# A chunked recurrence on five engines: loads moved to SyncE, six places for levels, a root by logarithm, sums in halves

## What is computed

```python
def step(state, xs):
    qt, kt, vt, bt = xs            # bt: cumulated log of the forget gate
    rel = jnp.where(tri, bt[:, :, :, None, :] - bt[:, :, None, :, :], -jnp.inf)
    att = jnp.einsum('bhtd,bhsd,bhtsd->bhts', qt, kt, jnp.exp(rel))
    o = jnp.einsum('bhts,bhsv->bhtv', att, vt) + \
        jnp.einsum('bhtd,bhdv->bhtv', qt * jnp.exp(bt), state)
    b_last = bt[:, :, -1:, :]
    new_state = jnp.exp(b_last[:, :, 0, :])[..., None] * state + \
        jnp.einsum('bhsd,bhsv->bhdv', kt * jnp.exp(b_last - bt), vt)
    return new_state, o
...
o_b = rms_norm(hgrn2(bq, bf, bi, lb_all[j]), b_out_norm_g[j])
o_b = o_b * jax.nn.silu(bg)
mix = jnp.concatenate([o_a, o_b], axis=-1) @ even_w_out[j]
x = x + mix
```

## Time and profile before

| what | us |
|---|---|
| median of 3 runs (2735.41 to 2735.88) | 2735.71 |
| the profiled execution, its own time | 2738.51 |
| its span in the profile | 2736.8 |
| TensorE busy (share of the span) | 2499.5 (91%) |
| VectorE busy | 1589.1 (58%) |
| GpSimd busy | 1353.6 (49%) |
| ScalarE busy | 1051.3 (38%) |
| from ScalarE's last attention copy to its first exponential of the loop (678.82 to 703.81) | 25.0 |
| first level to own projection (703.81 to 896.02) | 192.2 |

### The profile page before, as it was taken

The page is one execution under the profiler, slowest core; times in us unless marked ns, Lnnn a source line. Parts: engine busy times, 40 slices in busy tenths (PEclk is TensorE's granted clock), DMA queues, the critical chain, the costliest instruction groups (busy, mean ns, idle before and its releaser), DMA issues.

```text
span 2736.8 us, 31345 instructions
## 1 busy us (share of the span) xinstructions
PE 2499.5 (91%) x11111; PEld 1985.3 (73%) x11133; DVE 1589.1 (58%) x2354; ACT 1051.3 (38%) x1741; POOL 1353.6 (49%) x770
## 2 busy tenths in 40 slices
PE   6898897788577899999999989988998999999999
PEld 4677676444576678888888877766776888888887
DVE  6478668883677544455544654656534455544472
ACT  4255687555343422232322144525443232322220
POOL 4101234886555065566655913227524566655591
PEclk8999898799789999999999999988989999999999
DMA  4211123000300111122111212112002222111211
GB/s 147 50 28 28 31 66 93 12 10 3 123 9 8 31 55 38 61 62 61 47 38 38 74 73 73 45 33 81 9 16 62 62 61 61 46 39 38 61 54 69
DMA packets 164002, 136.57 MB, mean 50 GB/s; under 512 B 22969, under 2 KB 137730, under 8 KB 163906
## 3 DMA queue, kind: packets, MB, share of 16 engines
q1 hardware_dynamic: 143058, 116.19, 14.1%
q10 hardware_dynamic: 20848, 19.14, 2.4%
HBM read 116.17 MB, written 13.63 MB: 47 GB/s over the span
## 4 chain that ended last, share of the span: by engine, by line
PE 72%; DVE 9%; issue 8%; ACT 4%; POOL 3%; ACTq 1%; DMA 0%; another core or an unknown queue 0%; DVEq 0%; POOLq 0%
PE ps L2130 21%; PE ps L2132 21%; PE ps L2131 21%; ACT signs L1200 1%; POOL diag L824 1%; PE ps L2325 1%; PE ps L2242 1%; DVE ub L2023 1%; PE ps L2485 1%; POOL cl L874 1%; PE ps L2313 1%; PE ps L2333 1%; DVE ps L1709 1%; POOL w_lo L709 1%; DVE shared L2020 1%
## 5 line engine op out<-in xcount | busy, mean ns | idle before, releaser
L2130 PE MATMUL ps<-h_hi,w_hi 128*128 128x512 f32 x1680 | 671.6, 400 | 13.6 <-POOL w_lo L727 9.7
L2131 PE MATMUL ps<-h_lo,w_hi 128*128 128x512 f32 x1680 | 660.0, 393 | 0.0
L2132 PE MATMUL ps<-h_hi,w_lo 128*128 128x512 f32 x1680 | 659.5, 393 | 0.0
L2130 PEld LDWEIGHTS ps<-h_hi,w_hi 128*128 128x128 f32 x1680 | 319.9, 190 | 83.1 <-issue 14.4
L2131 PEld LDWEIGHTS ps<-h_lo,w_hi 128*128 128x128 f32 x1680 | 320.0, 190 | 68.2 <-issue 3.9
L709 POOL TENSOR_TENSOR w_lo<-w_raw,w_hi 128x1024 fp32r<-128x1024 f32 x73 | 182.6, 2501 | 377.3 <-ACT w_hi L1210 374.8
L2132 PEld LDWEIGHTS ps<-h_hi,w_lo 128*128 128x128 f32 x1680 | 319.1, 190 | 67.9
L2020 DVE TENSOR_TENSOR x_res<-ps,x_res 128x1024 f32<-128x1024 f32 x224 | 268.8, 1221 | 115.5 <-PE ps L2132 115.5
L2001 DVE TENSOR_TENSOR u_all<-ps,u_all 128x512 f32<-128x512 f32 x112 | 77.4, 691 | 415.9 <-ACT u_all L1107 415.9
L727 POOL TENSOR_TENSOR w_lo<-w_raw,w_hi 128x1024 fp32r<-128x1024 f32 x112 | 266.8, 2401 | 104.0 <-ACT w_hi L1096 104.0
L2130 PE MATMUL ps<-w_hi,uo_hi 128*128 128x512 f32 x784 | 307.5, 392 | 2.4 <-DVE shared L2020 2.4
(11 more groups left out here) (345 smaller groups left out, 4548.7 us busy)
## 6 DMA issues: line engine op xcount, KB each, us to landing
w_raw<-in_mlp_w_up SPq DMA_DIRECT2D x64, 512.0 KB, 4.0
w_raw<-in_mlp_w_down SPq DMA_DIRECT2D x64, 512.0 KB, 3.8
w_raw<-in_even_w_in SPq DMA_DIRECT2D x23, 512.0 KB, 3.8
w_raw<-in_odd_w_in SPq DMA_DIRECT2D x10, 512.0 KB, 3.7
x_res<-in_x SPq DMA_DIRECT2D x8, 512.0 KB, 8.1
x_res<-in_x ACTq DMA_DIRECT2D x8, 512.0 KB, 8.6
scr_x<-x_res SPq DMA_DIRECT2D x8, 512.0 KB, 2.6
x_res<-scr_x SPq DMA_DIRECT2D x8, 512.0 KB, 4.4
```

Source lines behind the costliest of these rows:

```text
L2130: t_.matmul(out_, ah, bh, start=first, stop=False)
L2131: t_.matmul(out_, ah, bl, start=False, stop=False)
L2132: return t_.matmul(out_, al, bh, start=False, stop=last)
```

## The change

- **Loads.** SyncE issues the value and gate loads and those of `x`, tiles 0 to 6, once the last attention values are multiplied and the sources are saved; tile 7 of `x` follows when all levels are done.
- **The last attention block** is divided in VectorE's slot 6, copied in ScalarE's slot 9, subtracted in GpSimd's slot 11. VectorE starts its loop when the attention's logits are done, TensorE at once.
- **Six places.** `RING` is 6: places 4 and 5 (`cl2`) lie where tile 7 of `x` goes. `READ_LAG` is 5.
- **Distances.** Output and state product at 4, root at 6, turn at 8, state at 9, gate at 12, high at 13, low at 14. `klT` is copied and `qe` made in the next chunk's first slots; the loop has 71 slots.
- **Root.** ScalarE makes four squares with an accumulated sum, Ln, Exp with scale -0.5, and the four scalings from bank 5, in one piece. VectorE's sum, reciprocal and norm are gone.
- **Sums.** The turned keys go to bank 7, so bank 4 holds only sums. Each of the 16 sums is made in two halves (6 matmuls) in adjacent slots; it is added four slots after its first half.

```diff
-        RING = 4
-        cl = at("cl", R_U, [P, RING, 512])
+        RING = 6
+        cl, cl2 = at("cl", R_U, [P, 4, 512]), at("cl2", R_X + 28 * KB, [P, 2, 512])
...
-        L_KL_ARG, L_KL_EXP, L_KL_PROD, L_KL_TURN, L_KL_COPY = 0, 2, 3, 4, 6
-        L_QE_EXP, L_QE_PROD, L_LAST, L_SPLIT = 4, 5, 6, 6
-        R_OUT, R_SQUARE, R_STATE, R_ROOT, R_NORM, R_TURN, R_GATE, R_HIGH, R_LOW = 1, 4, 5, 6, 7, 6, 9, 10, 11
-        READ_LAG = 3
+        L_KL_ARG, L_KL_EXP, L_KL_PROD, L_KL_TURN, L_SPLIT = 2, 3, 4, 5, 6
+        R_KL_COPY, R_QE_EXP, R_QE_PROD, R_LAST = 0, 2, 2, 4
+        R_OUT, R_ROOT, R_STATE, R_TURN, R_GATE, R_HIGH, R_LOW = 4, 6, 9, 8, 12, 13, 14
+        READ_LAG = 5
         HG_SLOTS = 7 * T + R_LOW + 1
+        LAST_NORM, LAST_HIGH, LAST_LOW = 6, 9, 11
...
-        OA_SLOTS = [7 * c + l for c in range(2, T) for l in (0, 2)] + [7 * T + l for l in (0, 2, 4, 5)]
-        OA_LAG = 3
+        OA_FIRST = [7 * c + l for c in range(2, T) for l in (-1, 2)] + [7 * T + l for l in (-1, 2, 5, 8)]
+        OA_PIECES = {n + k // 2: (i, (k, k + 1)) for i, n in enumerate(OA_FIRST) for k in (0, 2)}
+        OA_ADDS = {n + 4: i for i, n in enumerate(OA_FIRST)}
...
+            sp.wait_ge(att["pv_done"], len(TILES[0]))
...
+            for c in range(T):
+                sp.dma_start(chunk_values(o_sum, c), heads(scr_v[:, c, :])).then_inc(chunk_landed(c)[0], 16)
+                sp.dma_start(chunk_values(o_den, c), scr_g[:, :, c * P:(c + 1) * P]).then_inc(chunk_landed(c)[0], 16)
+            for t in range(T - 1):
+                sp.dma_start(x[:, t, :], a["x"][0, t * P:(t + 1) * P, :]).then_inc(x_landed[t], 16)
...
-            act.wait_ge(att["o_lo"], T)
-            act.wait_ge(b_ready, 8)
-            for c in range(T):
-                act.dma_start(chunk_values(o_sum, c), heads(scr_v[:, c, :])).then_inc(chunk_landed(c)[0], 16)
...
                 d = after_chunk(n, R_ROOT)
                 if d is not None:
-                    act.wait_ge(hg["o_ss"], d + 1)
-                    s.activation(sd[:, 0:4], ss[:, 0:4], ACT.Sqrt, scale=1.0 / P, bias=epsc[:]) \
-                        .then_inc(hg["o_sd"], 1)
+                    act.wait_ge(hg["s_done"], d + 1)
+                    for h in range(4):
+                        hs = slice(h * P, (h + 1) * P)
+                        ins = s.activation(kf[:, d, hs], ps[:, 5, hs], ACT.Square, accum_out=ss[:, h:h + 1])
+                    own.link(ins)
+                    own.link(s.activation(sd[:, 0:4], ss[:, 0:4], ACT.Ln, scale=1.0 / P, bias=epsc[:]))
+                    own.link(s.activation(rstd[:, 0:4], sd[:, 0:4], ACT.Exp, scale=-0.5))
+                    for h in range(4):
+                        ins = s.activation(chunk_values(o_sum, d)[:, h, :], ps[:, 5, h * P:(h + 1) * P], ACT.Identity,
+                                           scale=rstd[:, h:h + 1])
+                    ins.then_inc(hg["o_norm"], 1)
...
-            dve.wait_ge(att["o_lo"], T)
+            dve.wait_ge(att["st_done"], len(TILES[0]))
...
-                    v.tensor_reduce(ss[:, 0:4], heads(ps[:, 7, :]), AX_X, ALU.add).then_inc(hg["o_ss"], 1)
-                d = after_chunk(n, R_NORM)
...
-                            ins = t_.transpose(ps[:, 4, hs], ek[:, hs], ident[:])
+                            ins = t_.transpose(ps[:, 7, hs], ek[:, hs], ident[:])
...
-                    for k in range(4):
+                    for k in ks:
                         ins = products(ps[:, 4, :], (h_hi[:, k, ts_], h_lo[:, k, ts_]), (w_hi[:, k, cs], w_lo[:, k, cs]),
                                        k == 0, k == 3)
-                    ins.then_inc(down_done, 1)
+                    if ks[-1] == 3:
+                        ins.then_inc(down_done, 1)
```

More of the change, by code:

```diff
@@ L377, in after_chunk, with level @@
             return c if rem == 0 and 0 <= c < T else None
+        def level(n):
+            return (cl if n % RING < 4 else cl2)[:, n % RING % 4, :]
         def chunk_values(t, c):
@@ L855, in attention @@
                     u = ends_at(layer, n - ROUND[layer])
-                    if u is not None and u % 2:
+                    if u is not None and u % 2 and (layer or u // 2 < T - 1):
                         q = u // 2
@@ L865, in _ @@
             attention(0, PF0, PH0, PL0, diag0)
-            for n in range(7 * T):
+            last_block = block_outputs(0, T - 1)
+            for n in range(7 * T + R_QE_PROD + 1):
                 c, l = divmod(n, 7)
[L868 to L881, removed]
+                if n == LAST_LOW:
+                    pool.wait_ge(att["o_hi"], T)
+                    g.tensor_tensor(h_lo[last_block], o_den[last_block], h_hi[last_block].bitcast(F32), ALU.subtract) \
+                        .then_inc(att["o_lo"], 1)
+                if c < T:
+                    B = 1 << l
+                    e = level(n).rearrange("p (m s j) -> p m s j", s=2, j=B)
+                    pairs = kq[:, 0:2 * (KQ + B)].rearrange("p (s r) -> p s r", s=2)[:, :, c * 512:(c + 1) * 512]
+                    mixed = pairs.rearrange("p s (m j) -> p m s j", j=2 * B)[:, :, :, 0:B]
+                    pool.wait_ge(hg["exp"], 2 * n + 2)
+                    g.tensor_tensor(e, e, mixed, ALU.mult).then_inc(hg["prod"], 1)
+                    if l == L_KL_PROD:
+                        pool.wait_ge(hg["kl_exp"], c + 1)
+                        g.tensor_tensor(ek[:], ek[:], kf[:, c, :], ALU.mult).then_inc(hg["kl"], 1)
+                d = after_chunk(n, R_QE_PROD)
+                if d is not None:
+                    pool.wait_ge(hg["qe_exp"], d + 1)
+                    g.tensor_tensor(qe[:], qe[:], qf[:, d, :], ALU.mult).then_inc(hg["qe"], 1)
+                if l == L_SPLIT and 2 <= c < T and c % 2:
@@ L1324, in round_last @@
                 round_weights(U_OUT0 + 4 + i)
+            last_block = block_outputs(0, T - 1)
             for n in range(HG_SLOTS):
                 c, l = divmod(n, 7)
+                if n == LAST_HIGH:
+                    act.wait_ge(att["o_norm"], T)
+                    s.activation(h_hi[last_block], o_den[last_block], ACT.Copy).then_inc(att["o_hi"], 1)
                 if c < T:
-                    tk, B = slice(c * P, (c + 1) * P), 1 << l
-                    e = cl[:, n % RING, :].rearrange("p (b j) -> p b j", j=2 * B)
+                    B = 1 << l
+                    e = level(n).rearrange("p (b j) -> p b j", j=2 * B)
                     act.wait_ge(hg["diff"], n + 1)
@@ L1357, in _ @@
                     if d:
-                        act.wait_ge(hg["o_full"], d)
-                    s.activation(ps[:, 7, :], ps[:, 5, :], ACT.Square).then_inc(hg["o_sq"], 1)
+                        act.wait_ge(hg["s_done"], d)
+                    s.activation(klT[:], ps[:, 7, :], ACT.Copy).then_inc(hg["klT"], 1)
+                d = after_chunk(n, R_QE_EXP)
+                if d is not None:
+                    if d:
+                        act.wait_ge(hg["o"], d)
+                    s.activation(heads(qe[:]), bT[:, :, d * P:(d + 1) * P], ACT.Exp).then_inc(hg["qe_exp"], 1)
```

87 lines of the change are left out of this document (39 added, 48 removed).

## The result

| | us |
|---|---|
| median before (6 runs, 2735.41 to 2737.44) | 2735.84 |
| median after (6 runs, 2744.72 to 2747.28) | 2746.78 |
| ratio, 95% interval | 1.0038 [1.0025, 1.0051] |
| profiled execution after, its span | 2746.53, 2744.5 |

A forecast was written before the change was run, and what follows sets the result against it. Bound: a ring of hand-offs, no engine full. 705 + 24.3 + 5 x 30.2 + 30.0 = 910.3 against 896.0, +14.3 us, so 2752.8 profiled, less 2.8 for the median: 2750.0; own range 2739 to 2762, eight in ten 2722 to 2765.

The forecast's parts named there:

- The start, 25 us: Head of the recurrence: ScalarE's first exponential at 678.85 instead of 703.81, 25.0 us earlier; chunk 0's state product near 705.
- The chunk, 30.2 us: Chunks 2 to 6, from state product to state product: 30.2 us against 24.2 before, ends 28.1 and 32.6.
- the block, 6.9: ScalarE's squares, two table loads, Ln, Exp, scaling and `h_hi` in one piece: 6.9 us, 5.9 at the low end.
- `h_lo`, reading and VectorE's slots base+1 and base+2, 7.7: VectorE's work before TensorE's level of slot 7c (base): 1.5 us for `h_lo`, read and signal, then 6.2 for two slots.
- the hand-over, 4.65: TensorE's level base (slot 7c) and half sum, then VectorE's add, difference and read back to TensorE, serially: 4.65 us.
- the levels to the state product, 10.6: TensorE's levels base+1 to base+4 (base: slot 7c), turn, two half sums, output, state product, wait for gate: 10.6 us.
- Chunk 0 to 1: First spacing of state products, with no `h_hi` or `h_lo` in its way: 24.3 us with signals and restart.
- Chunk 6 to the own projection: From the last chunk's state product to the start of the out-projection proper: 30.0 us, against 30.9 before.
- The rival "no change": Root block short, a chunk takes 26.9 to 28.2 us, total within 5.5 us of nothing; chance 0.13.
- The lead: Rival: VectorE's lead half covers the block, chunks stay near 24 us, the start's gain remains, 2719 us; chance 0.18.
- No loads: Rival: exp and ln share a table, eight root blocks lose two 1.28 us loads each, 20.5 us, 2729.5; chance 0.03.
- The much slower case, by the clock: Rival: TensorE stands 7 us per chunk and its clock drops; chunk at 33 us, 2764 and beyond; chance 0.10.

The follow-up runs named there:

- the start alone: Kernel before, with only SyncE's loads and the last attention block's division, copy and subtraction in slots 6, 9 and 11: 2714.74 us, ratio 0.9921.
- the freed reading: Changed kernel with VectorE's `h_lo` put behind the reading of its slot instead of ahead of it: 2757.74 us, ratio 1.0069 to before.
- the fastest kernel: Changed kernel with ScalarE's root block one slot later and VectorE's addition of a half sum one slot later: 2694.74 us, ratio 0.9846 to before.
- the high half first: Changed kernel with `h_hi` ahead of the root block in ScalarE's slot: 2718.66 us, ratio 0.9953 to before.

## Why the prediction was right

**The bound.** A ring of hand-offs, no full engine: confirmed. VectorE's busy time per chunk fell by 3 us and the chunk got longer. TensorE's level waits 56.8 us for VectorE's reading and 5.9 for GpSimd's `cl`, which was one of the signs of being right.

**The start, 25 us.** ScalarE's first exponential came at 680.30, 1.5 us behind the predicted 678.85, which is the attention's own delay: the timeline has the copy at 679.69 (0.59 us) directly ahead. Chunk 0's state product ended at 707.7, or 706.2 less that delay, against 705. No load was waited for. The experiment with the start alone kept 21.6 us of the 25 (0.79%).

**The chunk, 30.2 us.** Measured 28.0 in the mean, 0.1 below the low end of 28.1, and the step that was mis-sized. By its terms:
- the block, 6.9: from 759.43 to 765.39 it is 6.0. I had taken four squares that don't overlap their reads, 2.0 us. Their starts lie only 0.25 to 0.27 us apart, and the four last 1.2 us: each read of 0.2 us runs beside the next square. The low end, 5.9, was the right one. Both loads are there, 1.28 us each.
- `h_lo`, reading and VectorE's slots base+1 and base+2, 7.7: end of the state product to level base is 13.4 to 13.5 us (788.54 to 801.92), against 6.9 + 1.5 + 6.2 = 14.6. Of the 1.2 us too much, 0.9 are the block; VectorE's slots took 5.8 us (796.13 to 801.92), not 6.2.
- the hand-over, 4.65: 801.92 to 806.57 is 4.65, to the digit.
- the levels to the state product, 10.6: 9.6 (806.57 to 816.14). The turn takes 0.44 us (807.56 to 808.00), not 0.89 like a level, and the 0.6 us of waiting for the gate don't show. It is 11.1 in the chunk from 759.23, whose matmuls ran longer at the lower clock (0.83 instead of 0.88). The 0.4 us added for restarts cover that in part.

**Chunk 0 to 1**, 24.3: measured 23.9. **Chunk 6 to the own projection**, 30.0: measured 33.3 (871.6 to 904.87). Here the clock was missing: TensorE stands 2.80 and 1.19 us ahead of the last sum, whose 12 matmuls then take 5.3 us (899.58 to 904.87) instead of the 2.85 taken: 2.4 of the 3.3 us.

**The sum.** 707.7 + 23.9 + 5 x 28.0 + 33.3 = 904.9, against the predicted 910.3: +2.7 at the start (of which 1.5 are the attention), -0.4, -11.0 for the chunks, +3.3 at the end. The direction was right since its reasons were: the serial chain behind the block and the hand-over each showed in an experiment of their own.

The size was in part luck. The rival "no change" had a block whose pieces overlap and a chunk of 26.9 to 28.2 us, and both are what was measured. With 28.0 us a chunk the prediction's own sum would be 910.3 - 11.0 = 899.3, only 3.3 us above before. The +2.7 at the start and the +3.3 at the end, neither of them foreseen, made it a clear loss. And the 2.8 us taken off between a profiled execution and the median did not hold for the changed kernel, whose two agree within 0.3 us: the profiled execution was 6.3 us below the forecast of 2752.8, the median only 3.2 below 2750.0.

**The rivals.** The lead doesn't hold. With `h_hi` ahead of the block the time is the 2719 that this rival had, though with chunks of 25.8 us and not of 24. No loads: refuted by the block's rows. The Trainium skill, "ScalarE: Activation LUTs", section "Table sets: the hidden batching unit", has ln and exp in one set; here each chunk loads once before Ln and once before Exp, 1.28 us each, and taking both away gave 20 us. The much slower case, by the clock, did not come: five chunks had 0.87 in the mean, against 0.89 before. Its mechanism exists: the experiment with the freed reading shows it at 0.78, and a chunk of 30.7 us.

## What to carry to other kernels

An engine that runs its list in order pays for a long piece of work with everything that stands behind it: for each block of several microseconds ask which short instruction behind it another engine waits for, and put that ahead, or the block behind the next stage's work. Moving a root block by one slot and an addition by one slot was worth 1.9% here, and turned a change that lost 0.4% into one that gains 1.5%. And a gain at the head of a ring is only kept if each pass stays as short as before.

## What was not expected

- A wait taken off one reading made the kernel 0.3% slower, since TensorE then stood later, twice ahead of level base for more than 2 us, and did more of its matmuls at the lower clock: the same eight matmuls take 1.06 us at 2.4 GHz and 2.08 us at 1.2 GHz. The Trainium skill, "TensorE: Matmul & The Clock Gate", section "HAM oscillation — how this bites in real kernels", describes a loop whose waits for DMA put TensorE back to the slow clock on every pass. These traces agree, with waits for other engines in place of DMA: behind the stand of 6.09 us the eight matmuls of after take 2.1 us in each of the five chunks, and the mean clock of a chunk is 0.78 with the stands of 4.41 and 2.97 us, 0.83 to 0.88 in after, and 1.00 in most chunks of the fastest kernel.
- What an edit gives must be looked for at the ends of the loop too: the high half first gained more behind chunk 6 (12.2 us) than in five chunks (10.8 us).
- The read of an accumulator (0.19 to 0.23 us) runs beside the next activation: four squares of 128 columns with their reads take 1.2 us.
